# A two-layer hybrid-attention inference step on one Trainium2 core: products of a constant where TensorE waits, two column groups of the first projection moved ahead of the gate logits, and another loop order for the new dilated scores

## The reference

```python
def decoder_layer(x, past_nsa, past_win, past_dil, ...):
    z = x @ w_in + b_in                      # 1024 -> queries, keys, values, gate logits, merge gates
    ...
    y_nsa = nsa_mixer(q_nsa, full, win, ...)         # compressed, selected and window attention, gated
    y_dil = dilated_mixer(q_dil, dil_all, ...)       # three groups of dilated windows, combined by softmax sums
    gm = sigmoid(g_merge)
    mixed = gm[0] * (y_nsa @ w_br_nsa) + gm[1] * (y_dil @ w_br_dil)
    x = layer_norm(ALPHA * x + mixed @ w_o, ln1_g, ln1_b)
    h = square(relu(x @ w_ff1))
    x = layer_norm(ALPHA * x + h @ w_ff2, ln2_g, ln2_b)
```

## Time and profile before

| what | value |
|---|---|
| median of three runs | 1488.45 us |
| the profiled execution: device time, span | 1487.74 us, 1486.0 us |
| TensorE busy with matmuls | 1413.0 us, 95% of the span |
| VectorE, ScalarE, GpSimd busy | 342.0, 307.9, 158.9 us |
| the chain that ended last, share by engine | TensorE 84%, SyncE's queue 5%, DMA 4%, VectorE 3%, ScalarE 2% |
| granted TensorE clock, mean over the span | 0.987 of 2.4 GHz |

### The profile page before, as it was taken

One profiled execution on the slowest core, in us unless ns is written; L12 is line 12 of the kernel. 1 busy time (PEld: TensorE's weight loads), 2 busy tenths in 40 slices (PEclk: granted clock), 3 DMA queues, 4 the chain that ended last, 5 costly groups with the idle time before them and its releaser, 6 DMA issues.

```text
span 1486.0 us, 23750 instructions
## 1 busy us (share of the span) xinstructions
PE 1413.0 (95%) x9098; PEld 1141.8 (77%) x9098; DVE 342.0 (23%) x887; ACT 307.9 (21%) x811; POOL 158.9 (11%) x268
## 2 busy tenths in 40 slices
PE   7999988999999999999999998899999999999996
PEld 4677767777769977777987777677776898777796
DVE  1222132344422311000122222324442221110002
ACT  1112242244310311000121223313432021100003
POOL 2100325000000000000300123420000000000000
PEclk9999999999999999999999999899999999999998
DMA  9999535596653666565945654467667447556640
GB/s 277 253 240 212 182 99 139 170 315 211 210 200 135 208 213 237 182 215 199 251 151 182 182 158 153 127 182 246 227 199 248 171 141 255 197 186 220 214 145 32
DMA packets 212771, 288.38 MB, mean 194 GB/s; under 512 B 14186, under 2 KB 201788, under 8 KB 211388
## 3 DMA queue, kind: packets, MB, share of 16 engines
q1 hardware_dynamic: 193573, 190.25, 42.8%
q10 hardware_dynamic: 9047, 71.53, 12.9%
q0 software_dynamic: 10048, 25.19, 6.4%
HBM read 277.03 MB, written 72.49 MB: 235 GB/s over the span
## 4 chain that ended last, share of the span: by engine, by line
PE 84%; SPq 5%; DMA 4%; DVE 3%; issue 2%; ACT 2%; DVEq 0%; ACTq 0%
PE psum L1632 76%; PE psum L1636 8%; DMA w_ring<-in_w_in 3%; SPq L506 1%; DMA yT<-in_cache_nsa_kv 1%; SPq L553 1%; SPq L578 1%; SPq L533 1%; SPq L521 0%; DVE pt L1503 0%; DVE logit L1394 0%; SPq L494 0%; SPq L501 0%; ACT xT L1213 0%; DVE logit L1559 0%
## 5 line engine op out<-in xcount | busy, mean ns | idle before, releaser
L1632 PE MATMUL psum<-arena,w_ring 128*128 128x144 f32 (+3 forms) x3584 | 679.5, 352 | 4.0 <-DVE arena L1610 2.3
L1632 PEld LDWEIGHTS psum<-arena,w_ring 128*128 128x128 f32 x3584 | 577.5, 190 | 106.7 <-issue 6.5
L1632 PE MATMUL psum<-xT,w_ring 128*128 128x288 f32 (+1 forms) x1472 | 362.4, 399 | 5.3 <-ACT kt L1152 3.1
L1632 PEld LDWEIGHTS psum<-xT,w_ring 128*128 128x128 f32 x1472 | 264.4, 190 | 79.5 <-issue 10.5
L1610 DVE TENSOR_TENSOR arena<-arena 128x288 f32 x64 | 29.3, 458 | 195.9 <-ACT arena L1225 195.9
L1225 ACT ACTIVATE arena<-psum 128x288 f32<-128x288 f32 x64 | 26.3, 411 | 193.3 <-PE psum L1632 193.3
L892 POOL TENSOR_TENSOR arena<-arena 128x144 f32<-128x144 f32 x24 | 11.7, 489 | 442.4 <-DVE arena L1605 441.3
L1636 PE MATMUL psum<-ident,regrouped 128*128 128x128 f32 x364 | 56.6, 287 | 1.8 <-ACT regrouped L945 1.4
L1636 PEld LDWEIGHTS psum<-ident,regrouped 128*128 128x128 f32 x364 | 45.0, 148 | 7.3 <-issue 3.2
L1306 DVE COPY arena<-psum 128x512 f32<-128x512 f32 x58 | 39.9, 690 | 32.4 <-PE psum L1636 30.7
L1614 DVE SCALAR_TENSOR_TENSOR arena<-arena,psum 128x288 f32<-128x288 f32 x12 | 4.9, 451 | 183.7 <-PE psum L1632 183.7
(11 more groups left out here) (248 smaller groups left out, 1170.8 us busy)
## 6 DMA issues: line engine op xcount, KB each, us to landing
w_ring<-in_w_ff SPq DMA_DIRECT2D x64, 1024.0 KB, 5.4
w_ring<-in_w_in SPq DMA_DIRECT2D x44, 1024.0 KB, 7.2
out<-in_cache_dil_w ACTq DMA_DIRECT2D x8, 1984.0 KB
w_ring<-in_w_o SPq DMA_DIRECT2D x8, 1024.0 KB, 7.7
out<-in_cache_nsa_win ACTq DMA_DIRECT2D x8, 992.0 KB
pages<-in_cache_nsa_kv POOLq DMA_DIRECT2D x32, 192.0 KB, 4.0
pages<-in_cache_nsa_kv SPq DMA_DIRECT2D x32, 192.0 KB, 5.1
arena<-in_cache_dil_w SPq DMA_DIRECT2D x46, 128.0 KB, 5.0
```

The source lines that it names most:

```text
L1632: return T.matmul(out, w, x, start=start, stop=stop, **kw)
```

## The change

Three things are done. TensorE multiplies the constant `ones` by itself: 16 times at the start, as soon as VectorE has written `ones`, into a part of bank 7 that nothing reads, and 12 times after the last `squares`, into bank 6. In layer 0 the groups i = 0 and 1 are computed, once all of `xT` is there, ahead of the transpose of the parameters and the gate logits. And the loop over the 48 products with the new rows has `pair` innermost instead of outermost.

```diff
+            def keep_busy(b, n):
+
+                for _ in range(n):
+                    mm(bank(b, 384, 128), ones[:, :], ones[:, :])
+
+            pe.wait_ge(s_su_d.sem, 1)
+            keep_busy(7, 16)
             pe.wait_ge(s_x.sem, 16 * 4)
             for k in range(KC):
                 for t in range(3):
...
+            def z_whole(l, i):
+
+                w_wait(l, f"z{i // 2}")
+                w = slot(i // 2 % W_SLOTS, KC, 256)
+                for k in range(KC):
+                    last = mm(bank(i % 2, 0, TOK), w[:, k, 128 * (i % 2):128 * (i % 2) + 128], xT[:, k], k == 0, k == KC - 1)
+                last.then_inc(z_mm.sem, 1)
...
             for l in range(layers):
-                if l:
+                if l == 0:
+                    pe.wait_ge(x_rdy.sem, x_rdy.after(0, 0))
+                    for i in range(2):
+                        z_whole(0, i)
+                else:
                     z_half(l, 0, 0)
...
                     if l and i < Z_FIRST:
                         z_half(l, i, 1)
-                    else:
-                        w_wait(l, f"z{u}")
-                        if i >= 2:
-                            pe.wait_ge(z_ev.sem, z_ev.after(l, i - 1))
-                        w = slot(u % W_SLOTS, KC, 256)
-                        for k in range(KC):
-                            last = mm(bank(i % 2, 0, TOK), w[:, k, 128 * (i % 2):128 * (i % 2) + 128], xT[:, k], k == 0, k == KC - 1)
-                        last.then_inc(z_mm.sem, 1)
+                    elif i >= 2:
+                        pe.wait_ge(z_ev.sem, z_ev.after(l, i - 1))
+                        z_whole(l, i)
...
-                for pair in range(4):
-                    for g in range(3):
-                        for par in range(2):
-                            for c in range(2):
+                for g in range(3):
+                    for par in range(2):
+                        for c in range(2):
+                            for pair in range(4):
                                 last = mm(bank(4, 384 + 32 * g, 32, 32 * pair, 32 * pair + 32), qd[:, pair, g, c, par],
                                           zf[:, KD + 2 * g + c, SEQ:TOK], False, True, skip_group_check=True)
...
             mean(layers - 1, 1, 1)
             squares(layers - 1, 1, 1)
+            keep_busy(6, 12)
             pe.wait_ge(x_rdy.sem, x_rdy.after(layers, 0))
```

More of the change, by code:

```diff
@@ L1770, in _ @@
                 for i, c in enumerate(Z_ORDER):
-                    u = i // 2
                     if l and i < Z_FIRST:
                         z_half(l, i, 1)
-                    else:
-                        w_wait(l, f"z{u}")
-                        if i >= 2:
-                            pe.wait_ge(z_ev.sem, z_ev.after(l, i - 1))
-                        w = slot(u % W_SLOTS, KC, 256)
-                        for k in range(KC):
-                            last = mm(bank(i % 2, 0, TOK), w[:, k, 128 * (i % 2):128 * (i % 2) + 128], xT[:, k], k == 0, k == KC - 1)
-                        last.then_inc(z_mm.sem, 1)
+                    elif i >= 2:
+                        pe.wait_ge(z_ev.sem, z_ev.after(l, i - 1))
+                        z_whole(l, i)
                     if i == 3:
```

## The result

The changed kernel takes 1501.6 us (median of 4 runs, 1499.82 to 1502.96) and the kernel before 1488.03 us (4 runs): a ratio of 1.0071, 95% interval 1.0037 to 1.0105. I had forecast 1495.0 us, with 1486 to 1500 as the range and "the same" as the likeliest verdict. The time lies 1.6 us above the range, and the better part of the interval is slower by more than 0.5%. The profiled execution took 1502.96 us, its span 1501.3 us, 15.3 us more than before.

The account below looks back on a forecast made before the run. TensorE was taken as bounding the kernel, level with the weight loads from 66 to 84 us. 1487.74 + 9.9 (lead) - 1.2 (scores) - 1.4 (end) = 1495.0 us, range 1486 to 1500.

Parts of the forecast that it names:

- The start: Up to i = 2: it starts at 25.2 to 26.6 us instead of 31.78, a lead taken as 5.5 us.
- What the lead does: Layer 0, i = 8 to 12: earlier table store delays window keys and z4; i = 12 starts 9.9 us later.
- the 18.9 us behind it: From z4's landing to i = 12: 16.7 us of TensorE time plus 2.2 us for restarting at half clock.
- the z4 term: Load z4, needed at i = 8, lands between 72.5 and 79.2 us, taken as 75.0.
- q10 and q1 have equal packet counts from 46 us on: Sign of being right: the table store's queue and SyncE's load queue take turns packet by packet.
- Shares by bytes: Rival, chance 0.15: queues share by bytes; z4 at 69 us, 3.9 us lost at i = 12, total 1489.0 us.
- q1 keeping its rate: Rival, chance 0.09: z4 lands at 66.46 us, only the clock costs 1.3 us, total 1486.4 us.
- the lead kept: Rival, chance 0.09: z4 lands by 61 us, the whole 5.5 us reaches the end, total 1479.6 us.
- The change doesn't do it: Rival, chance 0.07: start products don't raise the clock, i = 2 at 31 us, only scores gain, 1486.5 us.
- The 48 products: Scores of both layers: 96 records take 2.3 us, 0.6 us less per layer; gain 1.2 us, bounds 0 and 2.8.
- The end: Final transposes and copies: six copies take 3.6 us instead of 4.67 at full clock; gain 1.4 us.

Follow-up runs that it names:

- head_only: The kernel before with only the sixteen products at the start and i = 0 and 1 ahead of the gate logits: 1502.32 us, ratio 1.0112.
- store_later: The changed kernel with the table store issued two steps later in ScalarE's program, at i = 6: 1491.33 us, ratio 1.0019.
- before_flip: The kernel before with one more SyncE wait, holding layer 0's window keys until ScalarE is past the table store: 1502.72 us, ratio 1.0114.
- before_behind: The kernel before with layer 0's window-key loads issued behind z4 to z6, nothing else: 1482.56 us, ratio 0.9951.
- before_behind2: The kernel before with layer 0's window keys behind z4 to z6, run once more: 1482.70 us, ratio 0.9978.
- best: The kernel before with layer 0's window keys behind z4 to z6, new score order in layer 1 only, products at the end: 1480.04 us, ratio 0.9947.

## Why the prediction was right and wrong

*The start, right, with some luck.* i = 2 came 0.2 us after the end of the forecast stretch, the store 0.5 us after its figure. The prediction left open whether the clock lasts through the transposes. Here it did: the 32 records of i = 0 and 1, right behind them, take 8.03 us at a granted clock of 1.00. In `head_only` and `store_later` it did not, and they take 9.79 and 9.72 us.

*What the lead does, right in kind.* The store was pulled in front of the window keys, SyncE's queue slowed, TensorE stood before i = 8 and restarted at half speed (granted clock 0.50 from 81.6 to 84 us); `before_flip` shows that this order alone is enough, and `store_later` that z4 is in time without it.

*What the lead does, wrong in size.* The step that failed is the landing of z4: "Behind them z4 needs its own 8.7 us, or the 15.4 us that it had ... I take 75.0, a little under the middle." It landed at 81.5, and i = 12 came 6.0 us later than forecast, of the 8.0 us by which the sum of the terms is short. I worked it with 1024 packets behind the 2157, and more passed. The queues in the kernel before, from the store's beginning to the landing of z4 (51 to 66.5 us), which I had not counted:

```profile
q10 hardware_dynamic: 1281, 1.97, 47.0%
q1 hardware_dynamic: 1950, 1.80, 35.9%
```

2157 and 1950 are 4107 packets of q1 from 45.5 us to the landing of z4. The changed kernel, from 45.5 to its landing at 81.5 us:

```profile
q10 hardware_dynamic: 2801, 4.39, 50.0%
q1 hardware_dynamic: 4108, 3.18, 28.9%
```

4108 packets and 3.18 MB in both: the same work, in 36.0 us instead of 21. They are more than the window keys and z4. By size, before has 2048 packets of 512 bytes (the keys, 297 of them after 51 us), 312 of 1536 (page tiles), 135 of 4, and 1612 of 1024, where z4 has 1024: the other 588 belong to z5 and z6, which run ahead on the parts that the store leaves free (six parts of z5 land at 57.3 to 57.9 us). So the count is of what passes until z4 is whole, not of what stands ahead of it. The rate was forecast well, 118 packets/us against 114 measured. With the right count, 45.5 + 4107/118 gives 80.3 us, and with the 18.9 us behind it i = 12 at 99.2, where it came at 99.88. The upper end of the z4 term, 79.2, was the better guess, and I argued it down with the end of the store at 79. SyncE's 9.19 us for four issues, 2.17 before, I read as the same backlog seen from the issuing side; no row names what SyncE waits for there. I had said that z4's issue is not moved; it was, by 8.6 us. That the late issue costs nothing beyond the packets is argued from the count, not tested.

The sign "q10 and q1 have equal packet counts from 46 us on" did not come true: 2801 and 4108 up to the landing. They are equal in places (158 and 157 from 49 to 51 us), but q1 also runs on the six parts where the store has nothing.

*The rivals.* Shares by bytes (z4 at 69), q1 keeping its rate (66.46) and the lead kept (61) are all refuted by 81.5 us; bytes fail also with the right amount, 45.5 + 3.18/0.118 = 72.4. "The lead kept" fails even with the window keys out of the way: 64.1 us. "The change doesn't do it" had i = 2 at 31 us; it came at 26.79.

*The 48 products, wrong both ways.* I took 24 ns a record from wider products and forecast 0.6 us a layer. Without a stop a record takes 11 ns (96 in 1.05 us), a gain of 1.85 us a layer. But the faster run comes sooner to the place where the program is not there yet: 1.37 us in layer 0 without added products, 3.86 us in layer 1 with all of them, and a fallen clock for `fill(8)` behind the long one. That the added products move this place was not in the prediction at all; it cost 3.8 us in layer 1, where a gain of 0.6 stood.

*The end, right in kind, half in size:* 0.9 us in the changed kernel, 0.6 alone, of 1.4. The products hold the clock until the transposes begin, not through them.

The sum by its measured terms: 15.9 - 2.2 + 3.8 - 1.6 - 0.9 = 15.0 us of the 15.3. With z4 counted rightly (i = 12 at 99.2) and the rest as forecast, the prediction would have been 1487.74 + 15.2 - 2.6 = 1500.3 us and the verdict "slower".

*What stays open:* what SyncE waits for in its 9.19 us; why the store's packets took longer on sixteen engines than on ten; and part of what the keys behind gain alone. From the start of i = 2 to that of i = 12 all three profiled executions with that edit and no early start (`before_behind`, `before_behind2`, `best`) take 50.18 us, against 52.24 before, so 2.1 us stand there, more than the waits of 1.45 us in the rows of before. The medians say 4.5 us both times, with intervals of 3.1 to 11.3 and 0.7 to 5.9 us.

## What to carry to other kernels

Before an engine is let start earlier, list what its work triggers on other queues: here 5 us of lead put a store of 3840 KB ahead of 1024 KB of small packets that the next weights stood behind, and the cure was to change the order of issues, not the start. To cost a pinch of two queues, count in the trace of before the packets that pass up to the landing, also those of later loads, and divide by the rate of a stretch in which the two already share; in this one case, worked out afterwards, that gives the landing within 1.5 us. Filler products are also program: they shift the places where it must be fetched, and a run of very short instructions there can stop for longer than the reordering gains.

## What the hardware showed that I had not expected

Products of 32 columns that take turns over four column groups went at 11 ns a record (96 in 1.05 to 1.06 us), against 30 ns with twelve in a row in one group (2.90 us).

TensorE stopped at fixed places of its program: behind record 40 of layer 0 for 0 to 0.91 us with the slow order and 1.37 with the fast one, behind record 87 of layer 1 for 1.67 with the slow and 3.24 to 3.86 us with the fast one. It went on 1.29 to 1.55 us after a packet of q8 ended.

A load beside the store of 20 rows landed in six early parts and ten late ones, up to 18 us apart (z5 in the kernel before, 57.3 and 75.1 us).

Four single-row transfers in one queue took the whole core's DMA from 130 to 38 GB/s for over 20 us, with its engines busy for 0.89 of the time.
